# Second mixer: one product for the gate and the second values, later taps, and the convolution's sums in ring banks

## What is computed

```python
z = h @ w_in                      # 2 x 256 | 768 | 6 x 256 | 36 columns
a_conv, q, kc_r, vc_r, ks, vs, kw, vw, g = jnp.split(z, splits, axis=-1)

u, v = jnp.split(a_conv, 2, axis=-1)
y = u * jax.nn.sigmoid(v)
y = causal_depthwise_conv(y, w_dw) + b_dw         # 31 taps, 256 channels
conv_out = jax.nn.silu(layer_norm(y, ln_g, ln_b))

kc, vc = compress(kc_r, ...), compress(vc_r, ...) # 15 compressed positions
gates = jax.nn.sigmoid(g)                         # 12 heads x 3 branches
out = gates[..., 0] * o_c + gates[..., 1] * o_s + gates[..., 2] * o_w
x = x + jnp.concatenate([conv_out, out], -1) @ w_out
```

## Time and profile before

| | |
|---|---|
| median of three executions | 756.41 us (755.54 to 756.66) |
| the profiled execution | 756.39 us |
| its span | 754.6 us |
| mean granted clock of TensorE | 0.983 of 2.4 GHz |
| TensorE busy (weight loads) | 731.6 us, 97% (698.6 us, 93%) |
| VectorE busy | 510.7 us, 68% |
| ScalarE busy | 369.2 us, 49% |
| GpSimd busy | 80.2 us, 11% |
| DMA | 146.49 MB, 194 GB/s in the mean |

### The profile page before, as it was taken

How to read it: one execution, slowest core, us unless ns; L and a number is a source line. 1 busy time by engine, 2 the same in 40 slices (tenths; PEclk the granted TensorE clock), 3 DMA queues, 4 the chain that set the end, 5 groups by cost and what they waited for, 6 DMA issues and landing times.

```text
span 754.6 us, 13534 instructions
## 1 busy us (share of the span) xinstructions
PE 731.6 (97%) x5865; PEld 698.6 (93%) x5865; DVE 510.7 (68%) x612; ACT 369.2 (49%) x508; POOL 80.2 (11%) x74
## 2 busy tenths in 40 slices
PE   5899999999999999999999999999999999999996
PEld 4899999999999999999999999797799999998884
DVE  4998688788566777754447879974675666655361
ACT  3454434453644554553344565586854644444341
POOL 1500111003000000000004100005000232231001
PEclk9799999999999999999999979999999999999998
DMA  9989866887604777685560751333355656564611
GB/s 346 380 282 345 277 192 205 284 286 234 221 31 168 232 247 248 211 261 199 182 209 9 224 168 57 113 111 110 115 168 188 220 187 202 182 221 145 206 42 56
DMA packets 118335, 146.49 MB, mean 194 GB/s; under 512 B 4004, under 2 KB 103556, under 8 KB 118276
## 3 DMA queue, kind: packets, MB, share of 16 engines
q1 hardware_dynamic: 116912, 143.58, 57.7%
q10 hardware_dynamic: 1364, 2.05, 0.8%
HBM read 144.57 MB, written 1.05 MB: 193 GB/s over the span
## 4 chain that ended last, share of the span: by engine, by line
PE 74%; DVE 13%; ACT 6%; issue 4%; DMA 2%; POOLq 0%; SPq 0%; POOL 0%; DVEq 0%; ACTq 0%
PE bank L592 55%; PE bank L1081 8%; DVE w_lo L1516 6%; ACT w_hi L1120 4%; DVE mod_acc L1508 4%; PE bank L913 2%; DMA raw<-in_w_ada 2%; DVE wide L1786 1%; PE bank L877 1%; PE bank L879 1%; PE bank L652 1%; PE bank L629 1%; PE bank L857 1%; PE bank L896 1%; PE bank L950 1%
## 5 line engine op out<-in xcount | busy, mean ns | idle before, releaser
L1516 DVE TENSOR_TENSOR w_lo<-raw,w_hi 128x2048 fp32r<-128x2048 f32 x108 | 243.4, 2258 | 120.3 <-ACT w_hi L1120 120.0
L1120 ACT ACTIVATE w_hi<-raw 128x2048 fp32r<-128x2048 f32 x110 | 207.1, 1886 | 219.3 <-PE bank L592 167.6
L592 PE MATMUL bank<-act_hi,w_hi 128*128 128x256 f32 x816 | 227.5, 281 | 0.5 <-ACT act_hi L1277 0.2
L592 PE MATMUL bank<-act_lo,w_hi 128*128 128x256 f32 x816 | 225.2, 278 | 0.8 <-DVE act_lo L1575 0.5
L592 PE MATMUL bank<-act_hi,w_lo 128*128 128x256 f32 x816 | 221.7, 278 | 0.2 <-DVE w_lo L1516 0.2
L592 PEld LDWEIGHTS bank<-act_hi,w_hi 128*128 128x128 f32 x816 | 153.4, 188 | 3.5 <-issue 3.1
L592 PEld LDWEIGHTS bank<-act_lo,w_hi 128*128 128x128 f32 x816 | 153.3, 188 | 1.7 <-DVE act_lo L1575 0.7
L592 PEld LDWEIGHTS bank<-act_hi,w_lo 128*128 128x128 f32 x816 | 151.4, 188 | 0.4 <-DVE w_lo L1516 0.4
L592 PE MATMUL bank<-ffn_hi,w_hi 128*128 128x256 f32 x352 | 97.9, 278 | 0.0
L592 PE MATMUL bank<-ffn_hi,w_lo 128*128 128x256 f32 x352 | 97.3, 276 | 0.6 <-DVE w_lo L1516 0.6
L592 PE MATMUL bank<-ffn_lo,w_hi 128*128 128x256 f32 x352 | 97.2, 276 | 0.0
(11 more groups left out here) (274 smaller groups left out, 1096.8 us busy)
## 6 DMA issues: line engine op xcount, KB each, us to landing
raw<-in_w_in SPq DMA_DIRECT2D x31, 1024.0 KB, 6.3
raw<-in_w_ada SPq DMA_DIRECT2D x24, 1024.0 KB, 6.8
raw<-in_w_gate_up SPq DMA_DIRECT2D x22, 1024.0 KB, 5.1
raw<-in_w_mlp_in SPq DMA_DIRECT2D x16, 1024.0 KB, 5.3
raw<-in_w_mlp_out SPq DMA_DIRECT2D x16, 1024.0 KB, 5.3
raw<-in_w_down SPq DMA_DIRECT2D x10, 1024.0 KB, 5.1
raw<-in_w_out SPq DMA_DIRECT2D x8, 1024.0 KB, 6.8
raw<-in_w_proj_conv SPq DMA_DIRECT2D x2, 1024.0 KB, 5.4
```

The costliest lines, as they stand in the source:

```text
L592: i = e.matmul(dst, lhs, rhs, start=start and k == 0 and (m == 0 or second is not None) and n == 0, stop=stop and k == kt - 1 and n == 2, ...
L1120: e.activation(w_hi[slot][:, 0:kt * n_cols], raw[i % N_RAW][:, 0:kt * n_cols], ACT.Copy).then_inc(hi_split, 1)
L1516: e.tensor_tensor(w_lo[slot][:, 0:kt * n_cols], raw[i % N_RAW][:, 0:kt * n_cols], w_hi[slot][:, 0:kt * n_cols].bitcast(F32), ALU.subtract) ...
```

## The change

- The product `g` goes. `vw` moves from the steps to the end of `in2_first` and becomes a product of 292 streamed columns (256 of `vw`, 36 of `g`) from tiles of its own, `vwg_hi` and `vwg_lo`, that lie where `score` and `prob_more` come later. Its two token halves go to two banks. The gate's 144 KB come by a load of their own into `g_raw`, behind the raw tile of `vw`, after a wait on SP for the products before. ScalarE and VectorE split the joint tile in two instructions each; ScalarE evacuates gates, then values.
- `in2_heads` loses `vw`: `q1`, `kc` and the compress halves come one step earlier, `q2` is in step 5, and step 6 has no product.
- Taps: 2 ahead of `q0` and `vw`, none ahead of `ks` and `kw`, then 2, 2, 2, 4, 4, 5, 6 in the steps 0 to 6 and the last 2 in step 7.
- `mean` moves from step 6 to 7, `conv_norm` from 7 to 8, behind `c_scores`; the split of the convolution's result becomes a stage `conv_parts` in step 10. The sums use ring banks, the squares lie in `wide[1]`, and the waits for the shared bank go or change.

```diff
@@ -193,7 +193,12 @@
             rstd_col = alloc(own, "rstd_col", [P, TT])
+            with ExitStack() as before_heads:
+                g_raw = alloc(before_heads, "g_raw", [P, CHUNK_TILES, 3 * QH])
             score = [alloc(own, f"score{i}", [P, 6 * P]) for i in range(IN_FLIGHT)]
+            with ExitStack() as before_heads:
+                vwg_hi = alloc(before_heads, "vwg_hi", [P, CHUNK_TILES, CHUNK_COLS + 3 * QH], F32R)
+                vwg_lo = alloc(before_heads, "vwg_lo", [P, CHUNK_TILES, CHUNK_COLS + 3 * QH], F32R)
@@ -203,6 +208,7 @@
         conv_acc = wide[0][:, 4:4 + CT2, :]
+        conv_squares = wide[1][:, 0:CT2, :]
@@ -271,8 +277,8 @@
         assert QH * HD == 3 * CHUNK_COLS
-        in2_first = ("cu", "cv", "q0", "ks", "kw", "g")
-        in2_heads = ("vs", "vw", "q1", "kc", "w1k0", "w1k1", "q2", "vc", "w1v0", "w1v1")
+        in2_first = ("cu", "cv", "q0", "ks", "kw", "vw")
+        in2_heads = ("vs", "q1", "kc", "w1k0", "w1k1", "q2", None, "vc", "w1v0", "w1v1")
@@ -487,14 +494,16 @@
                     "q2": (q2_copied, 3), "ks": (ks_set, 1), "kw": (kw_set, 1), "vs": (vs_set, 1), "vw": (vw_set, 1),
-                    "g": (gate_set, 1), "kc": (cmp_scaled, 1), "vc": (cmp_scaled, 2)}
+                    "kc": (cmp_scaled, 1), "vc": (cmp_scaled, 2)}
...
                 banks.use("rstd", rstd_col_set, 1)
-        head_stages = {6: ("hidden0", "mean"), 7: ("keys", "conv_norm"), 8: ("c_scores",), 9: ("c_softmax",),
-                       10: ("hidden1",), 11: ("c_turn", "values"), 12: ("out0", "out1"), 13: ("out2", "out3"), 14: ("out4",)}
-        stage_free = {"hidden0": (cmp_hid_set, 2), "keys": (kc_set, 1), "c_scores": (c_copied2, 1), "c_softmax": (c_step, 2),
+        banks.use("vw1", *in2_free["vw"])
+        head_stages = {6: ("hidden0",), 7: ("keys", "mean"), 8: ("c_scores", "conv_norm"), 9: ("c_softmax",),
+                       10: ("conv_parts", "hidden1"), 11: ("c_turn", "values"), 12: ("out0", "out1"), 13: ("out2", "out3"), 14: ("out4",)}
+        TAPS_AT = (2, 2, 2, 4, 4, 5, 6)
+        stage_free = {"mean": (mean_set, 1), "conv_norm": (rms_set, 3), "hidden0": (cmp_hid_set, 2), "keys": (kc_set, 1), "c_scores": (c_copied2, 1), "c_softmax": (c_step, 2),
@@ -549,6 +558,9 @@
                 e.dma_start(raw_view(i), source.rearrange("(k p) c -> p k c", p=P)).then_inc(raw_landed[i % N_RAW], 16)
+                if i == product_at[VWG]:
+                    sp.wait_ge(product_done, IN2)
+                    e.dma_start(g_raw[:], in2["g"].rearrange("(k p) c -> p k c", p=P)).then_inc(g_landed, 16)
@@ -570,6 +582,8 @@
                 wl = w_lo[slot][:, 0:kt * n_cols].rearrange("p (k c) -> p k c", k=kt)
+                if p == VWG:
+                    wh, wl, n_cols = vwg_hi, vwg_lo, CHUNK_COLS + 3 * QH
@@ -584,7 +598,7 @@
                         if tokens_first:
-                            dst = o[:, m * n_cols:(m + 1) * n_cols]
+                            dst = o[:, m * n_cols:(m + 1) * n_cols] if second is None else (o, second)[m][:, 0:n_cols]
@@ -837,7 +851,8 @@
             for name in in2_first[2:]:
-                product(product_of[name], start_bank(name), *act2, tokens_first=(name == "g"))
+                product(product_of[name], start_bank(name), *act2, tokens_first=(name == "vw"),
+                        second=start_bank("vw1") if name == "vw" else None)
@@ -905,7 +920,10 @@
                     pe.wait_ge(cmp_paired_act, KV if not second else 2 * KV)
-                    pe.wait_ge(rms_set, 3 if second else 2)
+                    if second:
+                        pe.wait_ge(cmp_copied, 1)
+                    else:
+                        pe.wait_ge(rms_set, 2)
@@ -983,16 +1001,20 @@
             def conv_mean():
-                pe.wait_ge(cmp_copied, 1)
+                b = start_bank("mean")
...
                 for j in range(CT2):
-                    t = e.matmul(bank[SUMS][:, 0:T], ones[:], conv_acc[:, j, :], start=(j == 0), stop=(j == CT2 - 1),
+                    t = e.matmul(b[:, 0:T], ones[:], conv_acc[:, j, :], start=(j == 0), stop=(j == CT2 - 1),
...
             def conv_sums():
-                pe.wait_ge(mean_set, 1)
-                sum_tiles(range(CT2), True, True, (squared, 20 + CT2))
+                b = start_bank("conv_norm")
+                for j in range(CT2):
+                    pe.wait_ge(squared, 20 + j + 1)
+                    t = e.matmul(b[:, 0:T], ones[:], conv_squares[:, j, :], start=(j == 0), stop=(j == CT2 - 1),
+                                 skip_group_check=True)
+                t.then_inc(sums_done, 1)
@@ -1014,18 +1036,20 @@
                         cmp_softmax()
+                    elif stage == "conv_parts":
+                        pass
...
                         cmp_output(int(stage[3:]))
-                if h < len(in2_heads):
+                if h < len(in2_heads) and in2_heads[h]:
...
                     else:
-                        product(product_of[name], start_bank(name), *act2, tokens_first=name in ("vs", "vw"))
+                        product(product_of[name], start_bank(name), *act2, tokens_first=(name == "vs"))
@@ -1315,28 +1344,30 @@
                     e.activation(conv_s, conv_s, ACT.Sigmoid).then_inc(conv_sigmoid, 1)
-                elif name in ("vs", "vw"):
-                    act.wait_ge(product_done, p + 1)
-                    act.wait_ge(rstd_col_set, 1)
-                    v_, v_set = (vs_nat, vs_set) if name == "vs" else (vw_nat, vw_set)
-                    for tt in range(TT):
-                        t = e.activation(v_[:, tt, :], src[:, tt, :], ACT.Copy, scale=rstd_col[:, tt:tt + 1])
-                    t.then_inc(v_set, 1)
-                elif name == "g":
+                elif name == "vs":
...
                     for tt in range(TT):
-                        t = e.activation(gate[:, tt, :], b[:, tt * 3 * QH:(tt + 1) * 3 * QH], ACT.Sigmoid,
+                        t = e.activation(vs_nat[:, tt, :], src[:, tt, :], ACT.Copy, scale=rstd_col[:, tt:tt + 1])
+                    t.then_inc(vs_set, 1)
+                elif name == "vw":
+                    both = b, bank[banks.bank["vw1"]]
+                    act.wait_ge(product_done, p + 1)
+                    act.wait_ge(rstd_col_set, 1)
+                    for tt in range(TT):
+                        t = e.activation(gate[:, tt, :], both[tt][:, CHUNK_COLS:CHUNK_COLS + 3 * QH], ACT.Sigmoid,
...
                     preload(ACT.Exp)
+                    for tt in range(TT):
+                        t = e.activation(vw_nat[:, tt, :], both[tt][:, 0:CHUNK_COLS], ACT.Copy, scale=rstd_col[:, tt:tt + 1])
+                    t.then_inc(vw_set, 1)
...
                 act.wait_ge(sums_done, 3)
-                act.wait_ge(mean_set, 1)
-                e.activation(rms[:], bank[SUMS][:, 0:T], ACT.Sqrt, scale=1.0 / CH2, bias=eps[:, 0:1]).then_inc(rms_set, 1)
+                e.activation(rms[:], bank[banks.bank["conv_norm"]][:, 0:T], ACT.Sqrt, scale=1.0 / CH2, bias=eps[:, 0:1]).then_inc(rms_set, 1)
@@ -1395,8 +1426,7 @@
                             act.wait_ge(centred, j + 1)
-                            act.wait_ge(cmp_paired_dve, KV + 1)
-                            e.activation(squares[:, j, :], conv_acc[:, j, :], ACT.Square).then_inc(squared, 1)
+                            e.activation(conv_squares[:, j, :], conv_acc[:, j, :], ACT.Square).then_inc(squared, 1)
@@ -1513,6 +1544,11 @@
                 dve.wait_ge(hi_split, p + 1)
+                if p == VWG:
+                    e.tensor_tensor(vwg_lo[:, :, 0:n_cols], raw_view(i), vwg_hi[:, :, 0:n_cols].bitcast(F32), ALU.subtract)
+                    e.tensor_tensor(vwg_lo[:, :, n_cols:], g_raw[:], vwg_hi[:, :, n_cols:].bitcast(F32),
+                                    ALU.subtract).then_inc(lo_split, 1)
+                    return
@@ -1887,10 +1923,9 @@
                         dve.wait_ge(cmp_paired_dve, KV)
-                        dve.wait_ge(sums_done, 3)
...
                     pair_tokens(which, name[0:1])
-                if name not in ("cu", "cv"):
+                if name not in ("cu", "cv", "vw"):
@@ -1931,7 +1966,7 @@
                 dve.wait_ge(mean_summed, 1)
-                e.tensor_scalar(mean, bank[SUMS][:, 0:T], 1.0 / CH2, None, ALU.mult).then_inc(mean_set, 1)
+                e.tensor_scalar(mean, bank[banks.bank["mean"]][:, 0:T], 1.0 / CH2, None, ALU.mult).then_inc(mean_set, 1)
@@ -2022,7 +2057,7 @@
             for name in in2_first[2:]:
-                go_on(taps, 2)
+                go_on(taps, 2 if name in ("q0", "vw") else 0)
@@ -2034,7 +2069,9 @@
                     normalise(h - 1)
-                go_on(taps, 4 if h < 6 else TAPS2)
+                if h == 0:
+                    low_after(product_at[product_of["vw"]])
+                go_on(taps, TAPS_AT[h] if h < len(TAPS_AT) else TAPS2)
@@ -2046,7 +2083,7 @@
                         conv_norm()
-                    elif stage == "c_scores":
+                    elif stage == "conv_parts":
```

22 lines of the change are left out of this document (14 added, 8 removed).

## The result

The changed kernel took 766.19 us (median of 4 executions, 765.59 to 767.25), the kernel before 756.34 us (4 executions, 755.54 to 756.66): a ratio of 1.0121, 95% interval 1.0095 to 1.0148. It is 9.85 us slower. The forecast was 760.0 us with a range of 755.6 to 763.4: the direction was right, the size was not, and the time lies outside the range.

The account below looks back on a forecast made before the run. TensorE, busy 97% and slowed by the gate product's low clock, was taken as the bound, with VectorE late next. `vc` ending 0.70 us later plus 2.92 for the norm gave +3.6 on 756.39: 760.0 us, range 755.6 to 763.4.

Parts of the forecast that it names:

- TensorE's side: Gate product to `kc`: joint product 6.40 us at full clock, head 0's scores 1.41, `vs` 5.64, `kc` 5.84.
- the 5.96 set beside it: Joint product's length in us by the Trainium skill's issue-gap formula, 0.4 us below the forecast's own.
- the 9.63 us: Gain on TensorE alone from dropping the gate product and its low clock, if nothing else is late.
- VectorE is late next: From `kc` to the last tap VectorE needs 36.88 us, ending at 497.91; 0.98 of TensorE's gain is left.
- Rival 1: VectorE keeps up and TensorE's whole gain of 9.63 us comes through: 746.8 us; chance 0.10.
- The clock at `vc`: TensorE's idling brings the clock to 1.2 GHz when `vc` starts, costing 1.68 us; `vc` ends 0.70 later than before.
- the price of `vs` (1.68): Low-clock start cost: `vs` took 7.32 instead of 5.64 us before the change; the forecast charged this to `vc`.
- The norm behind the scores: ScalarE's norm chain, moved behind the compressed scores, makes the hidden values 2.92 us late, all let through.
- ScalarE's own lateness at the exponential: Moved norm chain brings ScalarE 1.30 us late to the exponential of the compressed softmax.
- this forecast: Clock low at `vc`, norm late, no block of VectorE by GpSimd: +3.6 us, 760.0 us; chance 0.40.
- rival 4: GpSimd's second w_out tile split blocks VectorE's compressed-softmax TENSOR_SCALAR up to 4.5 us, 2.9 left: 762.9 us; chance 0.20.
- it decides within half a microsecond which starts first: Rival 4's condition: GpSimd's split near 524.1 us against VectorE's TENSOR_SCALAR of the compressed softmax.

Follow-up runs that it names:

- the joint product alone: Changed kernel with the taps and the stages (mean, norm, convolution's copy) put back in their steps of before: 752.47 us, ratio 0.9938 to the kernel before.
- early taps: Changed kernel with the taps where they were before (2 ahead of q0, ks, kw, vw, then 4 per step), mean still in step 7: 759.66 us, ratio 1.0032.
- GpSimd later: Changed kernel, GpSimd beginning the low half of the second output-projection tile only after the last head's normalisation: 766.81 us, ratio 1.0119.
- the split early: Changed kernel, ScalarE making the high half of the second output-projection tile ahead of the stages of step 8: 761.26 us, ratio 1.0054.
- the kernels with the stages of before: Changed kernel with mean, norm and convolution's copy in their old steps, differing in taps or split place: ratios 0.9938, 0.9945, 0.9948, 1.0053.

## Why the prediction was wrong

- **TensorE's side: right.** Full clock at the joint product, 28.69 us from its start to the end of `kc` against 28.66. The joint product took 6.43 us (6.40 in the sum, and not the 5.96 set beside it), the scores of head 0 1.42 us; `vs` took 5.84 us instead of 5.64 and `kc` 5.65 instead of 5.84. That this is a real gain is shown by the joint product alone: 5.4 us of the first stretch, and 0.6% of the time. Of the other 4.2 of the 9.63 us, 2.9 are seen on its timeline of TensorE, even with early taps: 0.9 by which `vs` starts later behind the joint product (8.72 against 7.85 us, with a wait for `kw`), and waits of 0.45, 0.57, 0.53 and 0.45 us up to `vc`, all but the 0.53 (ScalarE's squares) for VectorE.
- **VectorE is late next: right.** Without a gap from 463.33 to the last tap; the mean's sums begin 66.07 us after the joint product, against 65.54 forecast. Rival 1 fell. Shown by taking the taps back (6.1 us) and by adding them alone (9.6 us).
- **The clock at `vc`: right, in part by luck.** +1.33 us in the first stretch against +0.70; 0.53 of the difference is the last tap, which came that much later than forecast. From the mean's sums to the end of `vc` it is 8.22 us against 8.12. But the parts differ: the step put the price of `vs` (1.68) wholly on `vc`, which took 6.71 us and not 7.34, while the mean's sums stand at the low clock too, 1.51 us from 500.51 to 502.02 instead of 0.78.
- **The norm behind the scores: right in size, in part by another way.** Without the hold, and with ScalarE's high half where the change has it, the hidden values come 2.66 us late (GpSimd later) against 2.92 forecast. With the split early 0.86 of the 1.88 us left are a thing that I put at nothing: the norm's sums (517.79 to 518.65 in the changed kernel) lie beside ScalarE's copy, as I said, but on TensorE the next compress half and the scores stand behind them. ScalarE's own lateness at the exponential is 0.95 us (21.12 against 20.17 behind the end of `vc`) and not 1.30.
- **What failed is the choice between this forecast and rival 4.** The sum put the meeting of GpSimd and VectorE at nothing. The mechanism, the instruction and the engine of rival 4 are what happened, and I gave them 0.20. Its price of 2.9 us for the hold was right (2.86), but it left out that the pause behind it brings the clock down once more: 1.04 us. So the 9.96 us are 3.62 forecast, 0.53 for the last tap, 0.10 at the mean and `vc`, -0.26 for the norm, 2.86 for the hold, 1.04 for the second low clock and 2.07 ahead of the joint product. The step in the text is "it decides within half a microsecond which starts first". That is true (it was 0.23 us), but it is the wrong question. GpSimd's split is 4.5 us long, and in such a time VectorE mostly comes to some instruction that can be held; the runs moved the split by -3.5 and by +15.7 us, and each time another one was hit, for 3.1 and 3.65 us. The places that cost next to nothing were VectorE's pause for the norm, where nothing is held, and those of the kernels with the stages of before, where 1.1 or 3.45 us are held off the path. My estimate of where the split starts (524.1) was early besides, since it left out the lateness of `vc`; with 1.33 and the 2.07 us it is 527.5, and 527.69 was measured.
- **The range** had no room for the execution itself. It was made against one profiled execution; the 2.07 us ahead of the joint product are outside of every term. Take them away and the changed kernel is at 764.1, still above 763.4; over the 762.9 of rival 4 the second low clock (1.04) is then the largest piece. Whether some of the 2.07 us belongs to the program stays open.

The Trainium skill, "SBUF — State Buffer", section on who interferes with whom, names copies and TENSOR_SCALAR as those that can contend with GpSimd, a TENSOR_TENSOR with both inputs in SBUF as one that contends when GpSimd reads SBUF, and TENSOR_REDUCE as one that doesn't on this chip. The traces agree: held were TENSOR_SCALAR of 4 and of 24 columns, `act_lo`, whose inputs lie in SBUF, and, by the split of the first w_out tile in the changed kernel (506.25 to 510.83 us), a COPY of 64x128 (1.30 us, where others take some 0.3); the reduction inside the split took its 0.69 us.
